# Two transformer blocks in one kernel: where the Strassen sums of the activations stand, and when GpSimd issues a load

## The reference, cut to what matters

```python
hf = rms_norm(x, g_ffn[layer])
x = x + (jax.nn.silu(hf @ w_gate[layer]) * (hf @ w_up[layer])) @ w_down[layer]
```

## Time and profile before

| | us |
|---|---|
| median of 3 runs | 2364.06 |
| lowest and highest | 2363.55, 2365.42 |
| the profiled execution | 2367.7 |
| its span, first to last instruction | 2365.9 |
| TensorE busy | 2352.9 |
| VectorE busy | 1948.9 |
| ScalarE busy | 1223.9 |
| GpSimd busy | 403.6 |

### The profile page before, as it was taken

How to read it: one execution, slowest core, us unless ns; L and a number is a source line. 1 busy time by engine, 2 the same in 40 slices (tenths; PEclk the granted TensorE clock), 3 DMA queues, 4 the chain that set the end, 5 groups by cost and what they waited for, 6 DMA issues and landing times.

```text
span 2365.9 us, 30942 instructions
## 1 busy us (share of the span) xinstructions
PE 2352.9 (99%) x10692; PEld 1957.8 (83%) x10692; DVE 1948.9 (82%) x2542; ACT 1223.9 (52%) x1639; POOL 403.6 (17%) x290
## 2 busy tenths in 40 slices
PE   9999999999999999999999999999999999999999
PEld 8988888878888788888888888888888888888887
DVE  7788887889888877878897976988988897787885
ACT  6554555645454544545654445455545454464553
POOL 1000000130534335200000000013053433520000
PEclk9999999999999999999999999999999999999999
DMA  8755455656766666665655564566575766665655
GB/s 304 238 176 186 153 170 167 222 196 189 248 203 233 204 228 226 213 213 187 195 196 196 178 196 160 194 239 204 186 251 198 242 213 236 216 214 200 212 190 168
DMA packets 130338, 487.44 MB, mean 206 GB/s; under 512 B 14480, under 2 KB 15120, under 8 KB 129568
## 3 DMA queue, kind: packets, MB, share of 16 engines
q1 hardware_dynamic: 116736, 421.32, 53.6%
q0 software_dynamic: 13184, 64.02, 7.6%
q10 hardware_dynamic: 288, 0.33, 0.0%
HBM read 483.51 MB, written 2.10 MB: 205 GB/s over the span
## 4 chain that ended last, share of the span: by engine, by line
PE 65%; DVE 3%; issue 0%; ACT 0%; ACTq 0%; DVEq 0%
PE acc L627 43%; PE po L627 7%; PE pt L627 6%; PE acc L774 3%; PE pt L774 2%; PE po L774 2%; DVE w_lo L1654 1%; DVE tmp_c L1789 1%; PE acc L664 0%; PE po L965 0%; PE acc L904 0%; PE acc L889 0%; PE po L973 0%; DVE tmp_b L1709 0%; ACT w_hi L1145 0%
## 5 line engine op out<-in xcount | busy, mean ns | idle before, releaser
L1654 DVE TENSOR_TENSOR w_lo<-raw,w_hi 128x1024 fp32r<-128x1024 f32 x796 | 1033.3, 1313 | 299.0 <-ACT w_hi L1145 292.2
L1145 ACT ACTIVATE w_hi<-raw 128x1024 fp32r<-128x1024 f32 x795 | 833.4, 1058 | 797.9 <-PE acc L627 499.2
L627 PE MATMUL acc<-w_hi,norm_hi 128*128 128x512 f32 (+1 forms) x1460 | 568.5, 390 | 0.1
L627 PE MATMUL acc<-w_hi,norm_lo 128*128 128x512 f32 (+1 forms) x1460 | 565.3, 387 | 0.0
L627 PE MATMUL acc<-w_lo,norm_hi 128*128 128x512 f32 (+1 forms) x1460 | 387.5, 387 | 0.0
L627 PE MATMUL acc<-w_hi,mix_hi 128*128 128x512 f32 x832 | 325.1, 391 | 0.8 <-DVE mix_lo L2153 0.8
L627 PE MATMUL acc<-w_hi,mix_lo 128*128 128x512 f32 x832 | 324.0, 389 | 0.0
L627 PEld LDWEIGHTS acc<-w_hi,norm_hi 128*128 128x128 f32 x1460 | 274.2, 188 | 55.8 <-issue 0.8
L627 PEld LDWEIGHTS acc<-w_hi,norm_lo 128*128 128x128 f32 x1460 | 274.2, 188 | 55.1
L627 PEld LDWEIGHTS acc<-w_lo,norm_hi 128*128 128x128 f32 x1460 | 272.9, 188 | 56.0 <-DVE w_lo L1654 0.2
L627 PE MATMUL acc<-w_lo,mix_hi 128*128 128x512 f32 x832 | 222.6, 389 | 0.2 <-DVE w_lo L1654 0.2
(11 more groups left out here) (354 smaller groups left out, 2934.8 us busy)
## 6 DMA issues: line engine op xcount, KB each, us to landing
raw<-stream SPq DMA_DIRECT2D x795, 512.0 KB, 3.7
heads<-seven_in POOLq DMA_DIRECT2D x48, 768.0 KB, 6.9
heads<-seven_in POOLq DMA_DIRECT2D x12, 512.0 KB, 7.4
tab<-seven_in POOLq DMA_DIRECT2D x12, 512.0 KB, 7.4
heads<-x_in POOLq DMA_DIRECT2D x4, 512.0 KB, 9.0
x<-x_tok POOLq DMA_DIRECT2D x4, 512.0 KB, 7.1
x<-mem_tok POOLq DMA_DIRECT2D x2, 1024.0 KB, 6.6
x<-x_tok POOLq DMA_DIRECT2D x1, 2048.0 KB, 10.1
```

The costliest lines, as they stand in the source:

```text
L627: last = pe.matmul(out_[:, c * NB:c * NB + width], a[:, k * T + c * P:k * T + (c + 1) * P], w[:, s, kk * width:(kk + 1) * width], start=cl ...
L1145: act.activation(w_hi[:, (units.fixed - 1) % RING, :], src, ACT.Copy).then_inc(w_hi_ready, 1)
L1654: dve.tensor_tensor(w_lo[:, s, :], src, w_hi[:, s, :].bitcast(F32), ALU.subtract)\
```

## The change

The activation sums stand in other pairs, and GpSimd issues the load of a pair's set 1 only when set 0 has landed.

- The norm sums move from (0, up, 1) to (0, up, 0). On VectorE the raw part comes behind the 13th split of the pair, the low part behind the 15th, ahead of `take_up`; on ScalarE the high part comes behind the 14th.
- The hidden sums of group 0 stay in (0, up, 2), those of group 1 move from (1, up, 2) to (1, up, 1) (`HIDDEN_SUMS`). The raw part stays behind step 9; the high part moves from ScalarE's step 10 to 13, the low part from VectorE's step 11 to 14, the last one, behind `take_up`.
- In (0, up, 1) the last low part of the tiles moves from VectorE's step 11 to 10.
- `load_seven` issues set 0 and the last tiles; `seven_sums` issues set 1 behind its wait for set 0, ahead of the subtractions on set 0.

```diff
+HIDDEN_SUMS = ((0, 2), (1, 1))
...
+            def load_set(j, step):
+                pool.dma_start(raw7(step, W11, 3), seven_in[j][:, step * 4 * NB:(step * 4 + 3) * NB])\
+                    .then_inc(seven_landed[step], 16)
+
             def load_seven(j):
-                for step in range(STEPS):
-                    pool.dma_start(raw7(step, W11, 3), seven_in[j][:, step * 4 * NB:(step * 4 + 3) * NB])\
-                        .then_inc(seven_landed[step], 16)
-                    if step == 0:
-                        pool.dma_start(last_raw(j), seven_in[j].rearrange("p (s n) -> p s n", s=STEPS)[:, :, 3 * NB:])\
-                            .then_inc(last_landed, 16)
+                load_set(j, 0)
+                pool.dma_start(last_raw(j), seven_in[j].rearrange("p (s n) -> p s n", s=STEPS)[:, :, 3 * NB:])\
+                    .then_inc(last_landed, 16)
...
                     pool.wait_ge(seven_landed[step], 16 * (j + 1))
+                    if step + 1 < STEPS:
+                        load_set(j, step + 1)
                     after_own(pool.tensor_tensor(raw7(step, T3), raw7(step, T2), raw7(step, T1), ALU.subtract), own + 1)
...
                             gated()
-                            split(3)
+                            split(1)
+                            sums_hi(False)
+                            split(2)
                             taken.add()
                             continue
                         if j is None:
-                            sums = {7: [gated], 9: [lambda: sums_hi(False)]}
-                            steps(2 * NU, both(early, preparing(after, 5, 6, 8), sums, joining(after, 13)))
+                            steps(2 * NU, both(early, preparing(after, 5, 6, 8), {7: [gated]}, joining(after, 13)))
                         else:
-                            sums = {10: [lambda: sums_hi(True)]} if p == 2 and g < LAST_GROUP else {}
+                            sums = {2 * NU - 3: [lambda: sums_hi(True)]} if (g, p) in HIDDEN_SUMS else {}
...
                             during(2 * NU - 3, at)
+                            sums_raw(False, which * N_SEVEN)
                             gated(2 * NU - 2)
                             split(2)
+                            sums_lo(False)
                             take_up(2)
                             split(1)
                             continue
...
                         if j is None:
-                            sums = {7: [lambda: sums_raw(False, which * N_SEVEN), gated],
-                                    10: [lambda: sums_lo(False)], 2 * NU - 1: [take_up]}
-                            steps(2 * NU, both(early, preparing(after, 6, 8, 11), joining(after, 13), sums))
+                            ends_ = {7: [gated], 2 * NU - 1: [take_up]}
+                            steps(2 * NU, both(early, preparing(after, 6, 8, 10), joining(after, 13), ends_))
                         else:
-                            sums, used = {}, which * N_SEVEN + (SEVEN.index((g, "up", 2)) if g < LAST_GROUP else 0)
-                            if p == 2 and g < LAST_GROUP:
-                                sums = {9: [lambda: sums_raw(True, used)], 11: [lambda: sums_lo(True)]}
+                            sums, used = {}, which * N_SEVEN + SEVEN.index(pair)
+                            if (g, p) in HIDDEN_SUMS:
+                                sums = {9: [lambda: sums_raw(True, used)], 2 * NU - 2: [lambda: sums_lo(True)]}
```

## The result

| | before | after |
|---|---|---|
| median of 17 runs, us | 2364.76 | 2368.75 |
| lowest and highest | 2361.76, 2367.61 | 2366.20, 2373.78 |
| ratio after / before, 95% interval | | 1.0022 [1.0015, 1.0029] |

The change makes the kernel slower: by the ratio 5.2 us, with an interval of 3.5 to 6.9 (the two medians lie 4.0 apart). I forecast 0.9 us faster. The time lies in the stated range (2356.5 to 2369.5), the direction is wrong.

The account below looks back on a forecast made before the run. TensorE bounds the kernel, busy 2352.9 of 2365.9 us. Added 10.1 less gone 11.0 gives net -0.9: 2367.7 becomes 2366.8, less 3.6 (profiled execution over median) 2363.2; range 2356.5 to 2369.5.

Parts of the forecast that it names:

- What goes: TensorE's losses at the (0, up, 1) products and near 780 and 1903 vanish once the sums leave: 11.0 us.
- 4.26 and 1.12 us: Losses near 780 and 1903 that go when the hidden sums leave (1, up, 2), in first and second feed-forward.
- My reading of the earlier trace: Near 780: ScalarE stood 5.25 us at the hidden sums, VectorE came late from (1, up, 2), TensorE waited 1.83 us.
- It costs 1.1 to 2.3 ... 1.1 back: (1, up, 1): hidden low part costs 1.1 to 2.3 us, 1.1 returns; TensorE loses 0.9 us first, 1.6 second.
- the freed meeting: (1, up, 1): GpSimd starting 0.56 us later frees one VectorE split of a meeting, 1.1 us back.
- the 1.45 us price: (0, up, 0): each small 128x256 norm sum on VectorE takes 1.45 us when it meets GpSimd's subtractions.
- the 4.4 us of lateness: (0, up, 0), first feed-forward: the norm sums make VectorE 4.4 us late, costing TensorE 3.6 us in pieces.
- Rival 1: Small sums in (0, up, 0) are not blocked, 0.3 us each: net -6.6 us, 2357.5; chance 0.28.
- rival 3: Set two late and nothing else moves, or old waits not the sums': within 1 us of before, 2364; chance 0.05.
- the first feed-forward's clock term: Behind the last wait after (0, up, 0), about 2 us, the half clock costs 1.7 us more.
- Rival 2: Half clock follows all four new waits, 6.8 us of loss: net +5.9, 2370.0; chance 0.15.
- The load: Set two's load issued when set one has landed: in time or up to 1 us late, costing nothing.

Follow-up runs that it names:

- second profile: The kernels before and after, each unchanged, profiled once more for one execution: 2363.47 us before, 2367.8 us after.
- e1: Kernel before with only the load order changed, set 1 issued behind set 0's landing: 1.0008 against before.
- e3: Kernel before with only the norm sums moved to (0, up, 0): 1.0017 against before.
- e10: Kernel before with the norm sums' move and the new load order, hidden sums unmoved: 1.0015 against before.
- e12: Kernel before with norm sums moved, low part in (0, up, 1), GpSimd's first subtractions four units later: 0.9983 against before.
- e5: Kernel before with only group 1's hidden sums moved to (1, up, 1), low part behind step 14: 1.0016 against before.
- e9: e8 with the load order of e1 added: 0.9974 against the kernel before, the fastest of all.
- e4: The changed kernel with GpSimd's first subtractions of each feed-forward four units later: 1.0006 against the kernel before.
- e2: The changed kernel with the old load order, so both moves of sums alone: 1.0033 against the kernel before.
- e11: Kernel before with group 1's hidden sums moved, but their low part only in (1, up, 2) behind step 9: 0.9994 against before.
- e8: Kernel before with the edits of e11 and e12 together, old load order: 0.9981 against before.

## Why the prediction was wrong

To see where each execution loses time, I compared when TensorE hands back each weight buffer, trace against trace. A step in the difference is what that stretch lost in all: idle time, refilling and clock together. The table gives these losses in us, counted from the trace that loses least in the stretch. The start of the program, where executions differ by up to 3.3, is left out.

| term | predicted | first profile | second profile |
|---|---|---|---|
| before: products of (0, up, 1), first and second | 4.26 + 1.35 | 4.30 + 1.26 | 4.27 + 1.28 |
| before: near 780 (and 820) | 4.26 | 4.19 + 0.45 | 0 |
| before: near 1903 | 1.12 | 0.82 | 0.80 |
| **sum that goes** | **11.0** | **11.0** | **6.4** |
| after: (0, up, 0), first | 5.3 | 4.95 | 3.35 |
| after: (0, up, 0), second | 2.3 | 2.61 | 2.59 |
| after: near 738, near 1863 | 0.9 + 1.6 | 1.89 + 2.08 | 1.99 + 1.86 |
| after: five smaller places | 0 | 2.5 | 1.2 |
| **sum that comes** | **10.1** | **14.0** | **11.0** |

In the mean of the profiles 12.5 come and 8.7 go: +3.8, for 5.2 measured in the times.

**The failed step is "What goes", its hidden part:** "4.26 and 1.12 us". The 4.26 were read rightly, but off one execution, and they are no fixed cost of the hidden sums' old place. Six profiles have the sums there. GpSimd's first subtraction and VectorE's first split behind the join start at:

| profile | subtraction | split | the two splits take | TensorE's wait behind them | stretch loses |
|---|---|---|---|---|---|
| before | 759.97 | 760.35 | 4.23 | 1.83 | 4.2 |
| before, second | 761.18 | 759.54 | 2.35 | none | 0 |
| e1 | 764.12 | 761.77 | 2.35 | none | 0 |
| e3 | 757.13 | 758.78 | 4.33 | 1.72 | 2.0 |
| e10 | 758.87 | 759.69 | 3.79 | 1.51 | 1.8 |
| e12 | 754.98 | 756.93 | 4.03 | 1.69 | 2.0 |

TensorE waits where the subtraction goes first, and only there. In the kernel before the half clock and the race lost one pair earlier came on top. The mean loss is 1.7 us, where my sum has 4.26. With 1.7 in it, 8.4 us go and the net is +1.7: the direction turns. (Near 1903 the six lose 0.8 to 1.9, in the mean 1.4, for 1.12.) The six are few, so this mean stays rough. My reading of the earlier trace rows falls as well: ScalarE stands 5.21 us for the sums in the second profile too, and TensorE doesn't wait. But the sums have a share: in the eight profiles with the hidden sums moved the first split starts ahead of the subtraction every time, and none loses over 0.3 there.

That the profiled execution took 3.6 us more than the median, which I subtracted at the end, was a weak warning. Of the twelve profiled executions whose kernel has a median, eleven lie above it, by 2.1 in the mean over all; e1's lies 2.6 above and began some 2 us late. Only the second profile and e1 showed which wait to doubt.

**"It costs 1.1 to 2.3 ... 1.1 back", near 738 and 1860,** was too small: 1.9 to 2.0 in place of 0.9, and 1.9 to 2.1 in place of 1.6. The price of the low part is right, the freed meeting isn't. With the term above, this step makes the rest of the error, together with the smaller places below. VectorE of the changed kernel there:

```profile
722.59 2.26 DVE L1659 TENSOR_TENSOR w_lo<-raw,w_hi 128x1024 fp32r<-128x1024 f32 x1
724.77 2.31 DVE L1901 TENSOR_TENSOR heads_r<-heads,heads_r 128x1024 fp32r<-128x1024 f32 x1
727.01 2.31 DVE L1659 TENSOR_TENSOR w_lo<-raw,w_hi 128x1024 fp32r<-128x1024 f32 x1
```

The low part is met (2.31 for 1.21), and so are the splits ahead of it and behind it, as before. GpSimd didn't start later, as I had it: counted from the load's first issue its first subtraction begins after 5.5 to 6.0 us in the two profiles of the change, after 6.1 to 7.1 in those of the kernel before. What brings the landing forward isn't shown.

**Right: the norm sums.** What goes at 510 and 1636 recurs in both profiles. The meeting, the 1.45 us price (1.40 measured) and the 4.4 us of lateness it led to came as worked out: 3.35 us for "3.6 in pieces", 2.6 for 2.3. Rival 1 is excluded by the rows, rival 3 by the old waits' absence. Only the first feed-forward's clock term is a matter of chance. Of the 26 waits of 1.49 to 1.87 us in the fourteen profiles of this case (behind the first 20 us), 5 were followed by a stretch at half clock, costing 1.6 to 1.7; of the 5 above 2.1 us, 4 were, and of the 11 from 0.99 to 1.42, none. So the 1.7 charged to one such wait should have been, by these counts, some 0.3 at each of the four.

**Rival 2** gave 2370.0, nearest in time, but that is luck, for its mechanism is wrong: one of four waits drew the clock down in the first profile, none in the second.

**Missed: the smaller places.** Ahead of (0, down, 1)'s products the same race is run. GpSimd and VectorE of e5 (first two fences), and of the kernel before (last two):

```profile
599.10 1.28 POOL L555 TENSOR_TENSOR heads<-heads 128x512 f32<-128x512 f32 x1 [4.39 <-DMA heads<-seven_in]
```
```profile
599.31 2.15 DVE L1655 TENSOR_TENSOR w_lo<-raw,w_hi 128x1024 fp32r<-128x1024 f32 x1
```
```profile
599.49 2.15 POOL L554 TENSOR_TENSOR heads<-heads 128x512 f32<-128x512 f32 x1 [4.84 <-DMA heads<-seven_in]
```
```profile
599.26 1.22 DVE L1654 TENSOR_TENSOR w_lo<-raw,w_hi 128x1024 fp32r<-128x1024 f32 x1
```

Where the subtraction is first by 0.21 us, the split ahead of the join takes 2.15 and TensorE waits 0.63; where the split is first by 0.23 us, it takes 1.22 and the subtraction pays.

**The load** was taken at nothing. Alone it measured +1.9 us, on the norm move -0.5, on both moves -2.6, on the best order -1.6, each known to about 3 us: nothing is still the best single value. It does move the race: the issue puts 0.56 us between set 0's landing and the first subtraction. In e1, e10 and both profiles of the change the waits near 602 and 1728 are 0.24 us or absent; but e9 has 1.24 at the first place and e4 1.32 at the second. Of the profiles with the old load order, four have 0.60 to 0.83 at both (e2, e3, e5, e11), e8 has 0.30 and 0.78, and e12 and both of the kernel before have none. Whether that is worth more than its price elsewhere stays open. Set 1 was late here and there, as bounded ("up to 1 us"): GpSimd's fifth subtraction at 809.57 in e9 waited 0.69 us for it.

## What to carry to other kernels

A wait in one profiled execution is a full term of the sum only if it belongs to the program. Take a second profile before you count it, and look at what released it a step further back: here a DMA whose landing helps to decide which of two engines goes first. Of an operation that is moved, each part has its own cover. The raw sums were harmless ahead of GpSimd's work (e11, e12). The low part, one operation in each feed-forward, cost some 5 us in all (e5 against e11) in the last steps of a pair, where sixteen transposes follow without a gap. Where two engines exclude each other, try first to move the one with slack out of the meeting: four units later took 3.8 us off the change (from the ratios 1.0022 and 1.0006, whose intervals just touch).

## What the runs showed of the hardware

A VectorE split that begins during GpSimd's DMA issue, with a subtraction queued right behind that issue, takes about what is left of both and its own work: 2.75 us, for 1.22 alone and 2.2 to 2.3 in an ordinary meeting. GpSimd and VectorE of the changed kernel:

```profile
932.01 0.56 POOL L538 DMA_DIRECT2D heads<-seven_in  x1 [4.84 <-DMA heads<-seven_in]
932.59 1.29 POOL L558 TENSOR_TENSOR heads<-heads 128x512 f32<-128x512 f32 x1
```
```profile
932.23 2.75 DVE L1659 TENSOR_TENSOR w_lo<-raw,w_hi 128x1024 fp32r<-128x1024 f32 x1 [1.49 <-ACT w_hi L1149]
```

The same at 676.58 (2.67 us) and in e9 at 596.47 (2.76), there the cause of e9's 1.24 us wait ahead of (0, down, 1)'s products. So in these rows a DMA issue set ahead of a subtraction widens the stretch in which VectorE loses the race. No run here separates the issue from the subtraction, so which of the two holds the port first isn't shown.
